# Split operands for the gate projections, and query norms moved into the exponential, in a two-block transformer kernel

## What is computed

```python
h = rms_norm_2(x, attn_norm_g[l])
c_q, c_kv, k_rope, gq, gk, gv, pool_in, gate_logits = split_columns(h @ w_in[l], IN_SIZES)
# mla: 8 heads of 96; q = rms(rms(c_q) @ w_uq), k = rms(concat(.. @ w_ukv, k_rope)), rope on both
# gqa: 8 query heads and 2 key heads of 64; rms per head, rope
sc = einsum(q, k) * dk ** -0.5 ; p = softmax(sc) ; o = p @ v
gates = sigmoid(gate_logits)            # three gates of 1024 columns
merged = sum(gates[b] * (o[b] @ w_branch[b]) for b in (mla, gqa, pool))
x = x + merged @ w_out[l]
x = x + (silu(conv(u)_gate) * conv(u)_val) @ ffn_w_down[l]     # u = rms(x) @ ffn_w_up[l]
```

## Time and profile before

| | |
|---|---|
| median of 3 runs | 2220.29 us (2218.03 to 2223.65) |
| the profiled execution | 2221.04 us, of which span 2219.2 us |
| mean granted TensorE clock | 0.988 |
| TensorE busy | 2108.8 us, 95% of the span |
| VectorE busy | 828.3 us, 37% |
| ScalarE busy | 539.8 us, 24% |
| DMA | 580.34 MB, mean 262 GB/s |

### The profile page before, as it was taken

How to read it: one execution, slowest core, us unless ns; L and a number is a source line. 1 busy time by engine, 2 the same in 40 slices (tenths; PEclk the granted TensorE clock), 3 DMA queues, 4 the chain that set the end, 5 groups by cost and what they waited for, 6 DMA issues and landing times.

```text
span 2219.2 us, 29739 instructions
## 1 busy us (share of the span) xinstructions
PE 2108.8 (95%) x11414; PEld 1321.7 (60%) x11415; DVE 828.3 (37%) x1534; ACT 539.8 (24%) x905; POOL 25.3 (1%) x45
## 2 busy tenths in 40 slices
PE   6998999999999999999999999999999999999999
PEld 4763333333333333333333787779999887688999
DVE  3522221122222112222122348433885258425874
ACT  1421111111111111111111122312663122403653
POOL 0000000000000000000000020000000020000000
PEclk9998999999999999999999999999999999999999
DMA  9696997099999999999899334316551633325551
GB/s 352 249 358 244 417 419 309 1 381 418 417 417 417 418 418 418 417 417 418 337 417 412 112 114 152 114 46 199 174 194 55 202 111 115 114 99 167 190 176 53
DMA packets 210550, 580.34 MB, mean 262 GB/s; under 512 B 23296, under 2 KB 125440, under 8 KB 174496
## 3 DMA queue, kind: packets, MB, share of 16 engines
q1 hardware_dynamic: 210464, 579.09, 68.0%
HBM read 577.74 MB, written 1.31 MB: 261 GB/s over the span
## 4 chain that ended last, share of the span: by engine, by line
PE 69%; DMA 11%; SPq 8%; DVE 8%; ACT 3%; issue 2%; ACTq 0%; DVEq 0%
PE bank L756 16%; PE bank L1016 13%; DMA ring<-in_w_gu 9%; PE bank L1067 8%; SPq L630 4%; SPq L632 3%; PE bank L1339 3%; PE bank L1341 3%; PE bank L1340 3%; PE bank L980 3%; PE bank L994 3%; DVE heap L2105 2%; PE bank L826 2%; DMA ring<-in_w_in 2%; PE bank L1355 1%
## 5 line engine op out<-in xcount | busy, mean ns | idle before, releaser
L1016 PE MATMUL bank<-ring,heap 128*64 128x512 f32 x2304 | 520.3, 601 | 29.5 <-DMA ring<-in_w_gu 29.5
L1016 PEld LDWEIGHTS bank<-ring,heap 128*64 128x64 f32 x2304 | 158.1, 138 | 373.7 <-issue 284.5
L756 PE MATMUL bank<-heap,ring 128*128 128x256 f32 (+1 forms) x1600 | 350.5, 380 | 5.3 <-DVE heap L2149 3.1
L756 PEld LDWEIGHTS bank<-heap,ring 128*128 128x128 f32 (+1 forms) x1600 | 301.0, 189 | 51.4 <-DVE heap L2149 4.0
L1940 DVE TENSOR_SCALAR heap<-bank 128x256 f32<-128x256 f32 x36 | 15.3, 425 | 731.5 <-PE bank L1016 731.5
L1067 PE MATMUL bank<-ring,heap 128*64 128x512 f32 x1152 | 255.1, 595 | 0.0
L1339 PE MATMUL bank<-h_hi,w_hi 128*128 128x256 f32 x640 | 181.7, 284 | 3.4 <-DVE w_lo L2162 3.4
L1340 PE MATMUL bank<-h_lo,w_hi 128*128 128x256 f32 x640 | 181.1, 283 | 0.0
L1341 PE MATMUL bank<-h_hi,w_lo 128*128 128x256 f32 x640 | 181.1, 283 | 0.0
L2162 DVE TENSOR_TENSOR w_lo<-ring,w_hi 128x2048 fp32r<-128x2048 f32 (+1 forms) x64 | 142.4, 2225 | 97.7 <-ACT w_hi L1634 97.7
L1067 PEld LDWEIGHTS bank<-ring,heap 128*64 128x64 f32 x1152 | 79.6, 137 | 149.9 <-issue 143.8
(11 more groups left out here) (297 smaller groups left out, 2289.4 us busy)
## 6 DMA issues: line engine op xcount, KB each, us to landing
ring<-in_w_gu SPq DMA_DIRECT2D x256, 1024.0 KB, 18.8
ring<-in_w_down SPq DMA_DIRECT2D x128, 1024.0 KB, 20.3
ring<-in_ffn_w_up SPq DMA_DIRECT2D x44, 1024.0 KB, 7.8
ring<-in_w_ada SPq DMA_DIRECT2D x24, 1024.0 KB, 10.6
ring<-in_w_in SPq DMA_DIRECT2D x24, 1024.0 KB, 7.9
ring<-in_ffn_w_down SPq DMA_DIRECT2D x16, 1024.0 KB, 6.0
ring<-in_w_in SPq DMA_DIRECT2D x7, 2048.0 KB, 12.2
ring<-in_w_out SPq DMA_DIRECT2D x6, 2048.0 KB, 13.2
```

The costliest lines, as they stand in the source:

```text
L756: last = mm(outp, w(k), x(k), start=k == 0, stop=k == nk - 1)
L1016: last = mm(psum[g][both[f], :], xgT[:, k % 4, k // 4, :], wt[:, g, :, f, :], start=False, stop=k == DT - 1, skip_group_check=True)
```

## The change

Six parts, all in the two layers.

1. The twelve gates go in split form. ScalarE writes `h_hi` once and `w_hi` for each gate (`lead_gate`), DVE `h_lo` and `w_lo` (`rest_gate`), and TensorE makes 48 products of fp32r operands for a gate where it made 16 of fp32. The slots are the two of the feed-forward part.
2. The root-mean-square factors of the queries no longer multiply the queries. They are computed with tokens over the partitions (`by_query`: the squares are the matmul's weights, a single column of ones or two of `pair` move), 16 columns for all heads, and enter as the per-partition `scale` of the exponential and in the row maximum's product. `ssq0..3` becomes `ssq`, and `ssg0`, `ssg1` become `ssgq`. The gain of the mla queries goes into the drain of `uq` on ScalarE, which makes the squares in the same place.
3. The order on each queue is new: mla sums of squares and `swq` come before the pool branch and `ga3` to `ga6`; the rotation of the gqa heads and of the keys comes after them; the rotation of the mla queries goes into the first attention steps on DVE.
4. The reciprocal of the keys' mean squares is taken in two pieces (5 and 3 heads), with the low parts `w_lo` of gates 5 and 6 between and behind.
5. `LRING` is 10240. The hi and lo tiles lie behind it, where they are live all through a layer. Loads are cut to pieces of at most 2048 columns for `w_gq`, `w_pool`, gates, branches and output projection. `w_gkv` now lies where `w_lat` lay, and waits for `ckv`; `up` pieces (4096 columns) alternate between two places.
6. `L["h"]` shares its place with `mq`, `xgain` with `mk`, the probabilities with `rs` and `sq`; banks 3 to 6 for `dn0..3`.

```diff
-LRING = 16384
+LRING = 10240
+MRING = 16384
+NG = 12
...
-        layer = [("w_lat", 8 * 416), ("w_gq", 8 * 512), ("w_gkv", 8 * 384), ("w_pool", 8 * 512), ("w_uq", 2 * 768),
-                 ("w_ukv", 1024), ("pool_w", 4 * P)] + [(f"gate{j}", 8 * 3 * 256) for j in range(4)] \
-            + [(f"br{b}", 4 * D) for b in range(3)] + [(f"wo{j}", 8 * 512) for j in range(2)] \
+        layer = [("w_lat", 8 * 416), ("w_gq0", 8 * 256), ("w_gq1", 8 * 256), ("w_gkv", 8 * 384), ("w_po0", 8 * 256),
+                 ("w_po1", 8 * 256), ("ga0", 8 * 256), ("ga1", 8 * 256), ("w_uq", 2 * 768), ("w_ukv", 1024), ("ga2", 8 * 256),
+                 ("pool_w", 4 * P)] + [(f"ga{n}", 8 * 256) for n in range(3, NG)] \
+            + [(f"br{b}{h}", 4 * 512) for h in range(2) for b in range(3)] + [(f"wo{i}", 8 * 256) for i in range(4)] \
...
+        def gate_unit(n):
+            hi, lo = (x[:, n % 2, :].rearrange("p (a b) -> p a b", a=DT) for x in (w_hi, w_lo))
+            return piece(lay_stream, f"ga{n}", DT), hi, lo
...
+            if name.startswith("ga"):
+                return S["wlo"], int(name[2:]) + 1
...
-                    if n % 3 == 0:
-                        arrived(f"gate{n // 3}")
-                    w = piece(lay_stream, f"gate{n // 3}", 8, 3)
+                    done("wlo", n + 1)
+                    _, hi, lo = gate_unit(n)
                     b = halves(lay(f"ga{n}"))
                     for a in range(2):
-                        last = product(b[:, a, :], lambda k: w[:, k, n % 3, P * a:P * (a + 1)], h, DT)
+                        for k in range(DT):
+                            wh, wl = hi[:, k, P * a:P * (a + 1)], lo[:, k, P * a:P * (a + 1)]
+                            mm(b[:, a, :], wh, h_hi[:, k, :], start=k == 0, stop=False)
+                            mm(b[:, a, :], wh, h_lo[:, k, :], start=False, stop=False)
+                            last = mm(b[:, a, :], wl, h_hi[:, k, :], start=False, stop=k == DT - 1)
                     last.then_inc(lay_full.sem, 1)
...
-                squares("ssg0", const("pair"), L["sq"], [(3, 1), (4, 1)])
-                squares("ssg1", const("pair"), L["sq"], [(5, 1), (6, 1)])
-                squares("ssgk", const("pair"), L["p"].rearrange("p a b -> p (a b)").rearrange("p (a b) -> p a b", b=T),
-                        [(0, 1), (1, 1)])
+                def by_query(name, slots, rows, sums):
+                    b = lay(name)
+                    n = 2 * NH // (TT * slots)
+                    for t in range(TT):
+                        for i in range(slots):
+                            o = NH * t + n * i
+                            last = mm(b[:, o:o + n], rows(i)[:, P * t:P * (t + 1)], sums, start=True, stop=True)
+                    last.then_inc(lay_full.sem, 1)
+                by_query("ssgq", 4, lambda i: L["sq"][:, 3 + i, :], const("pair").rearrange("p (a b) -> p a b", a=2)[:, :, 0])
+                squares("ssgk", const("pair"), L["gates"], [(0, 1), (1, 1)])
+                done("h1", 2)
...
+                drained_act("uq3")
+                by_query("ssq", NH, lambda i: L["sq"][0:MQ, i, :], const("ones", 1)[0:MQ, :])
+                gates(2)
+                done("ksq")
+                for i in range(4):
+                    squares(f"ssk{i}", const("ones")[0:MQ, 0:MQ], L["sq"], [(2 * i, 1), (2 * i + 1, 1)], MQ)
                 done("gn")
                 for i in range(2):
                     tiles_of(lay(f"swg{i}"), const("swap_g"), L["gq"], 2 * i, P).then_inc(lay_full.sem, 1)
                 tiles_of(lay("swgk"), const("swap_g"), L["gk"], 0, P).then_inc(lay_full.sem, 1)
+                for i in range(4):
+                    tiles_of(lay(f"swq{i}"), const("swap_m")[0:MQ, 0:MQ], L["mq"], 2 * i, MQ).then_inc(lay_full.sem, 1)
...
-                gates(2)
-                done("qsq")
-                for i in range(4):
-                    squares(f"ssq{i}", const("ones")[0:MQ, 0:MQ], L["sq"], [(2 * i, 1), (2 * i + 1, 1)], MQ)
-                gates(3)
-                gates(4)
-                done("ksq")
-                for i in range(4):
-                    squares(f"ssk{i}", const("ones")[0:MQ, 0:MQ], L["sq"], [(2 * i, 1), (2 * i + 1, 1)], MQ)
-                gates(5)
-                gates(6)
-                done("qn")
-                for i in range(4):
-                    tiles_of(lay(f"swq{i}"), const("swap_m")[0:MQ, 0:MQ], L["mq"], 2 * i, MQ).then_inc(lay_full.sem, 1)
+                for n in range(3, 7):
+                    gates(n)
...
+                def lead_gate(n):
+                    src, hi, _ = gate_unit(n)
+                    act.wait_ge(*lay_in.here(f"ga{n}", l))
+                    f(hi, src, ACT.Copy).then_inc(S["whi"].sem, 1)
                 def gates(n):
                     o = 8 * (n % 3) + 2 * (n // 3)
                     out_of(f"ga{n}", L["gates"][:, o:o + 2, :], func=ACT.Tanh, scale=0.5)
+                    if n + 2 < NG:
+                        lead_gate(n + 2)
...
-                    out_of(f"uq{i}", L["mq"][0:MQ, 2 * i:2 * i + 2, :], lambda b: two(b)[0:MQ])
+                    b = two(full(f"uq{i}"))[0:MQ]
+                    f(L["mq"][0:MQ, 2 * i:2 * i + 2, :], b, ACT.Identity, scale=v2("q_head", 0)[0:MQ])
+                    f(L["sq"][0:MQ, 2 * i:2 * i + 2, :], b, ACT.Square).then_inc(lay_drained["act"].sem, 1)
...
-                        scale = (MQ if att[i][0] == "m" else HD) ** -0.5
+                        scale = two(L["rq"][:, 0 if att[i][0] == "m" else 1, :])[:, :, int(att[i][1])]
...
+                ready("hhi", 1)
+                v.tensor_tensor(h_lo[:, :, :], L["h"], h_hi[:, :, :].bitcast(F32), ALU.subtract).then_inc(S["h1"].sem, 1)
+                def rest_gate(n):
+                    src, hi, lo = gate_unit(n)
+                    ready("whi", n + 1)
+                    v.tensor_tensor(lo, src, hi.bitcast(F32), ALU.subtract).then_inc(S["wlo"].sem, 1)
+                rest_gate(0)
...
+                rest_gate(1)
                 ready("lstd")
                 for k in range(2):
                     c.mark(scaled(L["cq"][:, k, :], v2("q_norm", k), L["rs"][:, 0, :]))
                 scaled(L["ckv"], v2("kv_norm", 0), L["rs"][:, 1, :]).then_inc(S["lat"].sem, 1)
+                rq = L["rq"]
+                taken(mean(rq[:, 1, :], full("ssgq")[:, 0:2 * NH], HD))
+                taken(mean(L["rs"][:, 6:8, :], two(full("ssgk")), HD))
+                own("ssgk")
+                c.mark(v.reciprocal(rq[:, 1, :], rq[:, 1, :]))
+                v.reciprocal(L["rs"][:, 6:8, :], L["rs"][:, 6:8, :]).then_inc(S["gvar"].sem, 1)
+                ready("gsq")
+                c.mark(v.tensor_scalar(L["gq"], L["gq"], v2("gq_head", 0), None, ALU.mult))
                 ready("gstd")
-                c.mark(scaled(L["gq"], v2("gq_head", 0), L["rs"][:, 2:6, :]))
                 scaled(L["gk"], v2("gk_head", 0), L["rs"][:, 6:8, :]).then_inc(S["gn"].sem, 1)
-                cos, sin = const("cos_g"), const("sin_g")
-                for i, name in enumerate(("swg0", "swg1", "swgk")):
-                    taken(v.tensor_tensor(L["rs"][:, 2 * i:2 * i + 2, :], two(full(name)),
-                                          sin.unsqueeze(1).to_broadcast([P, 2, T]), ALU.mult))
-                c.mark(v.tensor_tensor(L["gq"], L["gq"], cos.unsqueeze(1).to_broadcast([P, 4, T]), ALU.mult))
-                c.step(v.tensor_tensor(L["gk"], L["gk"], cos.unsqueeze(1).to_broadcast([P, 2, T]), ALU.mult))
-                own("swgk")
-                c.mark(v.tensor_tensor(L["gq"], L["gq"], L["rs"][:, 0:4, :], ALU.add))
-                v.tensor_tensor(L["gk"], L["gk"], L["rs"][:, 4:6, :], ALU.add).then_inc(S["rope_g"].sem, 1)
+                rest_gate(2)
+                taken(mean(rq[:, 0, :], full("ssq")[:, 0:2 * NH], MQ))
+                own("ssq")
+                v.reciprocal(rq[:, 0, :], rq[:, 0, :]).then_inc(S["qvar"].sem, 1)
+                rest_gate(3)
+                ready("gn")
+                for i in range(4):
+                    taken(mean(L["rs"][0:MQ, 2 * i:2 * i + 2, :], two(full(f"ssk{i}"))[0:MQ], MQ))
+                rest_gate(4)
+                own("ssk3")
...
+                turned("q", turned_q)
+                v.reciprocal(L["rs"][0:MQ, 0:5, :], L["rs"][0:MQ, 0:5, :]).then_inc(S["kvar"].sem, 1)
+                rest_gate(5)
+                v.reciprocal(L["rs"][0:MQ, 5:NH, :], L["rs"][0:MQ, 5:NH, :]).then_inc(S["kvar"].sem, 1)
+                rest_gate(6)
...
+                ready("kstd")
+                scaled(L["mk"][0:MQ], v2("k_head", 0)[0:MQ], L["rs"][0:MQ]).then_inc(S["kn"].sem, 1)
+                cos = const("cos_g")
+                c.mark(v.tensor_tensor(L["gq"], L["gq"], cos.unsqueeze(1).to_broadcast([P, 4, T]), ALU.mult))
+                c.mark(v.tensor_tensor(L["gk"], L["gk"], cos.unsqueeze(1).to_broadcast([P, 2, T]), ALU.mult))
+                rest_gate(7)
+                c.settle()
                 own("pl1")
-                ready("rope_g")
```

(80 more changed lines are left out.)

129 lines of the change are left out of this document (72 added, 57 removed).

## The result

The changed kernel takes 2185.32 us (median of 4 runs, 2183.34 to 2185.45) against 2219.89 us for the kernel before in the same session (4 runs, 2218.03 to 2223.65): a ratio of 0.9842, 95% interval 0.9826 to 0.9858. Forecast were 2184 us in a range of 2176 to 2196.

The account below looks back on a forecast made before the run. TensorE, busy 95% of the span, was taken to bound the kernel. The profiled 2221.0 us less 38.2 for two layers (19.1 each), plus 2 for gaps, gave 2184.8, so 2184 us for the median; range 2176 to 2196.

Parts of the forecast that it names:

- What sets the end: Whole kernel: TensorE is busy 95% of the span, so time comes from shorter TensorE work or its waits.
- Part 1, gates: Twelve gates a layer: split into 48 fp32r products, each takes 5.76 us instead of 6.91, saving 13.8 us.
- Part 2, query sums: Query sums of squares as one- or two-column fp32 matmuls: 48 records at 0.115 us, 5.5 us, a loss of 0.3.
- a rival: Clock falls in the one-column matmuls of `ssq`: 1.75 us a layer, 2187.5 us in all; chance 0.12.
- The two bounds beside it: Query sums' price a record: 0.06 us gains 2.6 us, 0.2155 us loses 5.1.
- Parts 3 and 4, waits: TensorE up to the fifth head's scores: waits of 0.9 us at gate 6 and 1.6 at gate 8, sum 2.5.
- The microsecond a layer taken off for gaps: Gain of 19.1 us a layer cut by 1 us for gaps between dependent instructions not laid out.
- Per-partition scale: Attention's exponential: the tiny extra operand costs nothing; bounds 0 and 0.1 us on 16 heads, 3 us in both layers.
- Part 5, loads: Ring loads closer to their readers: `w_gkv` lands after 9 us without wait; upper bound 19.8, a 6 us wait a layer.
- `up2`: Feed-forward load: issued at 1543.1, landing 1551.5, wanted by ScalarE at 1552.23; fits with 0.7 us.
- The later `up` pieces: Feed-forward loads in two places: 12.2 us left for landing, 7.8 in the median and 12.3 at most; fits.

Follow-up runs that it names:

- q_recip_back: The changed kernel with an unused 96x2048 reciprocal put back on VectorE behind the small query reciprocal: 2197.09 us, 0.990 of the kernel before.
- gates_fp32: The changed kernel with each gate again 16 fp32 matmuls, the product of the input's low part left out: 2209.56 us, 0.9965 of the kernel before.

## Why the prediction was right

- *What sets the end.* TensorE's queue, with VectorE's norms close behind it: right. The layer follows the sum of TensorE's records to a microsecond, and putting the VectorE work back costs what its order says (q_recip_back).
- *Part 1, gates.* 5.76 us forecast, 5.75 seen, and gates_fp32 gives 13.2 us a layer, 13.5 with the wait of 0.3, where 13.8 were put. The Trainium skill's four passes of true fp32 (FP8 and Floating Point Precision, TensorE Precision Notes) would have made a gate 5.18 us, as an estimate; the measurement decides, three split products take 0.83 of one fp32 product and not three quarters.
- *Part 2, query sums.* 0.115 us a record forecast, 0.109 seen. The price was right, and the clock wasn't in it. It was carried as a rival, 1.75 us a layer with a chance of 0.12. It came in one layer of the two, with 3.1 us, and in 12 of the 16 layers with these sums, at 1.5 to 3.1 us where TensorE set the pace: this is the term I mis-sized, its chance more than its price, and the likeliest case should have held some of it. The two bounds beside it mix their bases: "gains 2.6" counts from the 5.5 us taken, "loses 5.1" from the 5.2 us of the old sums; from the value taken it would be 4.8.
- *Parts 3 and 4, waits.* 2.5 us forecast (2.3 by the ends and due times given there, 0.85 and 1.45), 0.3 seen. Gate 6 waits 0.3 us where I had 0.9, and `w_lo` 8 ends at 1370.5, just as gate 8 starts at 1370.6, where I had it 1.6 us late. From the end of `w_lo` 6 to the end of `w_lo` 8 my layout took 17.6 us and VectorE took 16.3. It had no idle time there, and each of its rows starts some 0.08 us before the record ahead of it ends: the ten durations add up to 17.1 us, 0.7 more than they take. The microsecond a layer taken off for gaps wasn't there either: up to the fifth head's scores a layer without a fall gains 20.5 us, against 18.1 after the allowance.
- *Per-partition scale.* Put at nothing, bounds 0 and 0.1 us for each of 16 heads; it was 0.09 an exponential, two a head, and 1.04 us a layer came through. The upper bound of 3 us held for the sum of both layers, though not the 0.1 a head that it was made of; the value taken didn't hold.
- *Part 5, loads.* `gk` was on time: the four narrow loads of `w_gkv` issued in 2.83 us and landed in 3.2 to 5.1 each, and the fifth landed 8.6 us after the first was issued, against my 9 and a bound of 19.8. A sign that the 12.38 us of the earlier trace rows came from the queue ahead and not from the loads; no run tests it. `up2`, with 0.7 us in hand by my sum, landed after 9.1 us in place of 7.8 in layer 0 and made unit 4 0.64 us late; in layer 1 it was no later than before. The later `up` pieces were in time.

```profile
1250.03 2.83 SPq L709 DMA_DIRECT2D ring<-in_w_in  x4
1252.90 1.37 SPq L711 DMA_DIRECT2D ring<-in_w_in  x1
```

The sum for the profiled execution was 2184.8 us and 2185.4 came, with errors that cancel: 2.4 us a layer too little gain in waits and gaps, and 2.1 in a first block that happened to be shorter, against 1.04 a layer for the scale, 3.1 for the clock in layer 1 and 2.1 at unit 4. The large terms were right; that the sum comes within 1 us of the measured time is luck.

## What to carry to other kernels

Here an fp32 matmul cost the same with 1 and with 128 moving columns, with the weight loads running all the time beside it (3.49 of 3.50 us in the window at 1316), and with 128 the clock stayed up in all four layers. So where a narrow matmul has spare columns for nothing, try them and look at the granted clock of the stretch behind it. When an operation becomes cheaper on one engine and dearer by a tenth of a microsecond on another, ask whether that one lies in a chain from engine to engine; idle time beside it is no cover. And where the gain rests on operands that another engine prepares, write down that engine's order with due times: here it gave the price of the two pieces of VectorE work that were put back to within a microsecond a layer (2.5 for 2.8, 8.0 for 8.5).
